# Weight pieces laid out by the host in load order for a two-layer decoder trunk on one core

## The reference

```python
for layer in range(DEPTH):                       # DEPTH = 2
    y = _rmsnorm(h, norm_mix_g[layer])
    h = h + _hybrid_mixer(y, w_in[layer], b_igate[layer], ..., w_out[layer])
    y = _rmsnorm(h, norm_ffn_g[layer])
    if layer % 2 == 0:
        h = h + _swiglu(y, ffn_w_gate[0], ffn_w_up[0], ffn_w_down[0])     # 1024 -> 2752 -> 1024
    else:
        h = h + _moe_swiglu(y, w_router[0], moe_w_gate[0], moe_w_up[0], moe_w_down[0])  # 8 x 1024 -> 3584 -> 1024
return _rmsnorm(h, norm_final_g)

def _swiglu(h, w_gate, w_up, w_down):
    return (jax.nn.silu(h @ w_gate) * (h @ w_up)) @ w_down
```

## Time and profile before

| | |
|---|---|
| median of 3 runs | 1499.48 us (1499.21 to 1503.12) |
| the profiled execution | 1500.5 us, its span 1498.7 us |
| mean granted TensorE clock | 0.989 |
| TensorE busy (matmul) | 1452.7 us, 97% |
| VectorE, ScalarE busy | 1136.4 us (76%), 1005.1 us (67%) |
| HBM read | 434.77 MB |
| SP's queue | 182928 packets, 429.94 MB |

### The profile page before, as it was taken

How to read it: one execution, slowest core, us unless ns; L and a number is a source line. 1 busy time by engine, 2 the same in 40 slices (tenths; PEclk the granted TensorE clock), 3 DMA queues, 4 the chain that set the end, 5 groups by cost and what they waited for, 6 DMA issues and landing times.

```text
span 1498.7 us, 20052 instructions
## 1 busy us (share of the span) xinstructions
PE 1452.7 (97%) x7604; PEld 1237.5 (83%) x7604; DVE 1136.4 (76%) x864; ACT 1005.1 (67%) x827; POOL 33.3 (2%) x62
## 2 busy tenths in 40 slices
PE   5999999999999899999999999999999999999997
PEld 5898899997898688888888888888888888888775
DVE  4456644445455778888888888888888888888997
ACT  4568534435567657777777777777777777777765
POOL 4000000000000010000000000000000000002000
PEclk9999999999999989999999999999999999999999
DMA  9633455554533469999999999999999999999993
GB/s 349 242 115 113 168 171 195 168 183 152 170 114 113 150 252 386 365 377 390 386 371 380 391 367 379 393 370 384 392 373 374 386 376 381 386 375 385 394 365 121
DMA packets 189553, 445.96 MB, mean 298 GB/s; under 512 B 9512, under 2 KB 11560, under 8 KB 189504
## 3 DMA queue, kind: packets, MB, share of 16 engines
q1 hardware_dynamic: 182928, 429.94, 78.9%
q0 software_dynamic: 3344, 11.09, 2.0%
q10 hardware_dynamic: 3232, 4.26, 0.8%
HBM read 434.77 MB, written 10.49 MB: 297 GB/s over the span
## 4 chain that ended last, share of the span: by engine, by line
PE 88%; ACT 4%; DVE 4%; issue 2%; DMA 1%; ACTq 0%; DVEq 0%
PE ps L1374 81%; PE ps L1751 2%; ACT whi L511 2%; DVE wlo L905 1%; DMA wif<-in_w_in_dram 1%; ACT L521 1%; PE ps L1521 1%; PE ps L1393 1%; DVE y L927 0%; PE ps L1721 0%; PE ps L1718 0%; PE ps L1534 0%; DVE y L1092 0%; ACT qkc L685 0%; PE ps L1523 0%
## 5 line engine op out<-in xcount | busy, mean ns | idle before, releaser
L905 DVE TENSOR_TENSOR wlo<-raw,whi 128x2048 fp32r<-128x2048 f32 x405 | 926.1, 2291 | 283.7 <-ACT whi L511 281.8
L511 ACT ACTIVATE whi<-raw 128x2048 fp32r<-128x2048 f32 x405 | 776.9, 1919 | 388.0 <-PE ps L1374 382.6
L1374 PE MATMUL ps<-whi,xT_hi 128*128 128x512 f32 x1056 | 417.7, 396 | 2.2 <-DVE wlo L905 2.2
L1374 PE MATMUL ps<-wlo,xT_hi 128*128 128x512 f32 x1056 | 411.8, 390 | 0.0
L1374 PE MATMUL ps<-whi,xT_lo 128*128 128x512 f32 x1056 | 411.1, 389 | 0.0
L1374 PEld LDWEIGHTS ps<-whi,xT_hi 128*128 128x128 f32 x1056 | 198.4, 188 | 43.0 <-issue 3.2
L1374 PEld LDWEIGHTS ps<-wlo,xT_hi 128*128 128x128 f32 x1056 | 198.2, 188 | 42.4
L1374 PEld LDWEIGHTS ps<-whi,xT_lo 128*128 128x128 f32 x1056 | 198.5, 188 | 38.9
L1374 PE MATMUL ps<-whi,hid_hi 128*128 128x512 f32 (+1 forms) x536 | 210.9, 393 | 0.8 <-DVE hid_lo L1224 0.8
L1374 PE MATMUL ps<-wlo,hid_hi 128*128 128x512 f32 (+1 forms) x536 | 208.9, 390 | 0.0
L1374 PE MATMUL ps<-whi,hid_lo 128*128 128x512 f32 (+1 forms) x536 | 208.8, 389 | 0.0
(11 more groups left out here) (247 smaller groups left out, 776.1 us busy)
## 6 DMA issues: line engine op xcount, KB each, us to landing
raw<-in_moe_w_gate_dram SPq DMA_DIRECT2D x112, 1024.0 KB, 7.4
raw<-in_moe_w_up_dram SPq DMA_DIRECT2D x112, 1024.0 KB, 7.5
raw<-in_moe_w_down_dram SPq DMA_DIRECT2D x112, 1024.0 KB, 7.3
raw<-in_w_in_dram SPq DMA_DIRECT2D x28, 1024.0 KB, 5.6
raw<-in_ffn_w_gate_dram SPq DMA_DIRECT2D x10, 1024.0 KB, 5.1
raw<-in_ffn_w_up_dram SPq DMA_DIRECT2D x10, 1024.0 KB, 5.1
raw<-in_ffn_w_down_dram SPq DMA_DIRECT2D x10, 1024.0 KB, 4.8
raw<-in_w_out_dram SPq DMA_DIRECT2D x8, 1024.0 KB, 4.9
```

The costliest lines, as they stand in the source:

```text
L511: act.activation(whi[:, i % NSPLIT, :], raw[:, i % NRAW, :], ACT.Copy).then_inc(hi_ready, 1)
L905: dve.tensor_tensor(wlo[:, i % NSPLIT, :], raw[:, i % NRAW, :], whi[:, i % NSPLIT, :].bitcast(F32), ALU.subtract).then_inc(lo_ready, 1)
L1374: ins = pe.matmul(acc, lhs, rhs, start=start and m == 0, stop=stop and m == 2, skip_group_check=True)
```

## The change

The host builds one more input, `w_pieces`, of 405 pieces of 128 x 2048 float32 in the order in which they are loaded. Each piece is laid out as the buffer `raw` wants it, so a load reads 128 rows of 8 KB that lie behind one another in HBM. Input `w_in` stays, because `wif` is still cut from it. The output, feed-forward and expert matrices are no longer inputs of the device program. The two short pieces become full ones, and the last piece of the dense layer is loaded by one transfer instead of two.

```diff
-            def load(i, parts):
+            def load(i, at=None):
                 if loop.reg is not None or i >= NRAW:
                     sp.wait_ge(lo_ready, loop.at("piece", i - NRAW + 1))
-                for place, src in parts:
-                    sp.dma_start(place, src).then_inc(arrived[i % NRAW], 16)
-            def cols(i, w, half, c0, n=FB):
-                v = raw[:, i % NRAW, :].rearrange("p (k n) -> p k n", k=4)
-                rows_ = w[half * 512:(half + 1) * 512, bass.ds(c0, n)]
-                load(i, [(v, rows_.rearrange("(k p) n -> p k n", p=P))])
...
+                src = w_pieces[i] if at is None else \
+                    w_pieces[bass.ds(at, 1)].rearrange("o p n -> (o p) n")
+                sp.dma_start(raw[:, i % NRAW, :], src).then_inc(arrived[i % NRAW], 16)
             for t in range(TT):
                 sp.dma_start(h[:, t, :], x[0, t * P:(t + 1) * P, :]).then_inc(x_in[t], 16)
-            mixer(0)
...
-            mixer(1)
+            for i in range(MOE_BASE):
+                load(i)
             def job(e, next_rows=False):
...
+                for i in range(JOB_PIECES):
+                    load(MOE_BASE + i, e * JOB_PIECES + (MOE_BASE + i))
+                    if i == JOB_PIECES // 2 and next_rows:
                         sp.wait_ge(x_sent, 16 * 2 * TT)
                         sp.wait_ge(xg_ps, loop.at("half", 2))
                         sp.dma_start(x_slots, x_by_slot[bass.ds((e + 1) * P, P), :]
...
 def arrival(i, loop):
-    last = FFN_BASE + FFN_PIECES - 1
-    more = 16 if i >= last and (i - last) % NRAW == 0 else 0
-    n = 16 * (i // NRAW + 1) + more
+    n = 16 * (i // NRAW + 1)
...
+def pieces_of(w_in, w_out, ffn_w_gate, ffn_w_up, ffn_w_down, moe_w_gate, moe_w_up, moe_w_down):
+    out = np.zeros((MOE_BASE + E * JOB_PIECES, P, PIECE), np.float32)
+    def cols(i, w, half, c0):
+        out[i].reshape(P, 4, FB)[:] = \
+            w[half * 512:half * 512 + 512, c0:c0 + FB].reshape(4, P, FB).transpose(1, 0, 2)
+    def two_rows(i, w, r0):
+        out[i].reshape(P, 2, D)[:] = w[r0:r0 + 256].reshape(2, P, D).transpose(1, 0, 2)
...
```

More of the change, by code:

```diff
@@ L85, with trunk @@
 DUMP = E * P
-def trunk(nc, x, norm_mix_g, w_in, b_igate, b_fgate, conv_w, conv_b, g_mlstm, g_sb, w_out,
-          norm_ffn_g, ffn_w_gate, ffn_w_up, ffn_w_down, w_router, moe_w_gate, moe_w_up,
-          moe_w_down, norm_final_g, out):
+def trunk(nc, x, norm_mix_g, w_in, w_pieces, b_igate, b_fgate, conv_w, conv_b, g_mlstm, g_sb, norm_ffn_g, w_router,
+          norm_final_g, out):
     x_by_slot = nc.dram_tensor("x_by_slot", (DUMP + 2 * TT * P, D), F32, kind="Internal").ap()
@@ L355, in _ @@
-            load(n, [(v[:, 0], wd[c0:c0 + P, :]), (v[:, 1], wd[F_DENSE - P:, :])])
-            mixer(1)
-            def job(e, next_rows=False):
[L359 to L372, removed]
+            for i in range(MOE_BASE):
+                load(i)
@@ L376, in job @@
                                      ).then_inc(x_slots_in, 16)
-                for half in range(2):
-                    two_rows(n + down_piece(EB - 1, half, EB), expert(moe_w_down),
-                             (EB - 1) * FB + 256 * half)
             with sp.Fori(0, E - 1) as j:
@@ L1840, in arrival @@
 def arrival(i, loop):
-    last = FFN_BASE + FFN_PIECES - 1
-    more = 16 if i >= last and (i - last) % NRAW == 0 else 0
-    n = 16 * (i // NRAW + 1) + more
+    n = 16 * (i // NRAW + 1)
     return n if loop.reg is None else loop.reg * (16 * (loop.per["piece"] // NRAW)) + n
-_INS = ['x', 'norm_mix_g', 'w_in', 'b_igate', 'b_fgate', 'conv_w', 'conv_b', 'g_mlstm', 'g_sb',
-        'w_out', 'norm_ffn_g', 'ffn_w_gate', 'ffn_w_up', 'ffn_w_down', 'w_router', 'moe_w_gate',
-        'moe_w_up', 'moe_w_down', 'norm_final_g']
+def pieces_of(w_in, w_out, ffn_w_gate, ffn_w_up, ffn_w_down, moe_w_gate, moe_w_up, moe_w_down):
+    import numpy as np
+    out = np.zeros((MOE_BASE + E * JOB_PIECES, P, PIECE), np.float32)
[4 more added lines that the diff above has]
+        out[i].reshape(P, 2, D)[:] = w[r0:r0 + 256].reshape(2, P, D).transpose(1, 0, 2)
+    for l in range(DEPTH):
+        for b in range(BLOCKS):
+            for half in range(2):
+                cols(MIX_BASE[l] + 2 * b + half, w_in[l], half, FIRST_COLUMN[b])
+        for i in range(4):
+            two_rows(MIX_BASE[l] + 2 * BLOCKS + i, w_out[l], 256 * OUT_PIECES[i])
+    wg, wu, wd = ffn_w_gate[0], ffn_w_up[0], ffn_w_down[0]
+    for f in range(DENSE_FULL):
+        for half in range(2):
+            cols(FFN_BASE + gate_piece(f, half), wg, half, f * FB)
+            cols(FFN_BASE + gate_piece(f, half) + 2, wu, half, f * FB)
+            if f < DENSE_FULL - 1:
+                two_rows(FFN_BASE + 8 + 6 * f + half, wd, f * FB + 256 * half)
+    n = FFN_BASE + 6 * DENSE_FULL - 2
+    c0 = DENSE_FULL * FB
+    for w in (wg, wu):
+        out[n, :, :KC * TAIL].reshape(P, KC, TAIL)[:] = w[:, c0:].reshape(KC, P, TAIL).transpose(1, 0, 2)
+        n += 1
+    for half in range(2):
+        two_rows(n, wd, c0 - FB + 256 * half)
+        n += 1
+    out[n, :, :D], out[n, :, D:] = wd[c0:c0 + P], wd[F_DENSE - P:]
+    for e in range(E):
+        n = MOE_BASE + e * JOB_PIECES
+        for f in range(EB):
+            for half in range(2):
+                cols(n + gate_piece(f, half), moe_w_gate[0, e], half, f * FB)
+                cols(n + gate_piece(f, half) + 2, moe_w_up[0, e], half, f * FB)
+                two_rows(n + down_piece(f, half, EB), moe_w_down[0, e], f * FB + 256 * half)
+    return out
@@ L1853 @@
+_INS = ['x', 'norm_mix_g', 'w_in', 'w_pieces', 'b_igate', 'b_fgate', 'conv_w', 'conv_b', 'g_mlstm',
+        'g_sb', 'norm_ffn_g', 'w_router', 'norm_final_g']
+_WEIGHTS = ['w_in', 'w_out', 'ffn_w_gate', 'ffn_w_up', 'ffn_w_down', 'moe_w_gate', 'moe_w_up',
+            'moe_w_down']
 def kernel(**inputs):
@@ L1859 @@
     arrays, args = {}, []
+    inputs = dict(inputs)
+    inputs["w_pieces"] = pieces_of(*(np.asarray(inputs[k]) for k in _WEIGHTS))
     for name in _INS:
```

## The result

| | before | after |
|---|---|---|
| median | 1499.51 us (4 runs, 1499.21 to 1503.12) | 1516.92 us (4 runs, 1514.88 to 1517.25) |
| profiled execution, its span | 1500.5 us, 1498.7 us | 1514.88 us, 1513.1 us |

The changed kernel takes 1.0108 times as long (95% interval 1.009 to 1.0126), which is some 16 us; the medians lie 17.4 us apart. The forecast was 1516.

The account below looks back on a forecast made before the run. The start was taken as the bound, where TensorE waits on the chain behind `wif`, not the experts. `wif` 16.6 us late plus 0.5 us of clock made 17.1, 1516.6 from the median 1499.5, stated as 1516; range 1507 to 1521.

Parts of the forecast that it names:

- What bounds the kernel: TensorE is busy throughout the experts, so faster transfers shorten nothing there; the start remains, where the chain waits for `wif`.
- The turn: In the DMA engines: one packet from each busy queue in turn, whatever its size; an 8 KB row as one packet, 0.50.
- the rival of two packets of 4 KB: Each 8 KB row goes as two packets: `wif` 14.6 us late, 15.1 with the clock, 1514.6 us; chance 0.33.
- The price: Start, 7 to 17 us: a turn with an 8 KB packet takes 0.333 us, 30 turns, leaving q10 95 packets per engine.
- the mean engine: Turn arithmetic at the start: an average engine finishes q10's packets at 38.1 us after the change, 20.4 before.
- the tail: Slowest engine at `wif`'s landing: half of the earlier 2.2 us added to 38.1, giving 39.2, so `wif` 16.6 us late.
- The clock: TensorE's restart after a 19 us pause: extra loss bounded by 0 and 1.7 us, taken as 0.5.
- Piece 0: First weight piece at the start: lands 0.3 us sooner, worth nothing because TensorE waits later for piece 1 anyway.
- The store of a job's result: In the experts, on q10: lands 1.9 us later, after 8.1 us, with ScalarE free to wait at 10.3; counted 0.
- The sum: Whole kernel: 16.6 us from late `wif` plus 0.5 of clock, 17.1 us; from the median 1516.6, stated as 1516.
- the first products of the experts: Sign in the profile after: the experts' first 512-column work starts later by the same as TensorE's idle, some 19 us.
- The rival on the faster side: Small queue gets more turns, `wif` lands before about 18 us, no pause after piece 0: 4.5 us gained, 1495.0; chance 0.04.

Follow-up runs that it names:

- two other kernels with a pause of 17 to 18 us: The kernel before with its first seven pieces in 8 KB rows, 1517.41 us; the changed kernel with contiguous pieces in 4 KB rows, 1514.4 us.
- four kernels that do land there: Changed kernel with SP holding from piece 2, 1494.22 us; with first seven pieces in 1 KB rows, 1495.7; with packed `wif`, 1495.27; kernel before with packed `wif`, 1495.14.

## Why the prediction was right

The mechanism held at every step, and the sizes were close; the terms that were off are named below.

*What bounds the kernel.* The experts did not care: an expert's stretch stayed as it was, and loading 398 of 405 pieces in the new way changed nothing that can be told.
*The turn.* One packet of each busy queue in turn, whatever its size: 565 to 566, 229 to 231 to 230. That an 8 KB row is one packet, which no row of before could show, is shown by the count of 59904; the rival of two packets of 4 KB is out, and the run with real 4 KB rows gave the 1514.4 that was worked out for it (1514.6), though its `wif` was used at 36.4 us where I had 37.2, and its clock made up for that.
*The price.* I had q10 with 95 packets left per engine at 17 us; it had (2224 - 222 - 566) / 16 = 90. The turn was 160 / 565 = 0.283 us, not 0.333, and q10 and q1 passed 35 packets per engine in that stretch, not 30. I had left out that each transfer closes with one short packet per engine, so that one in nine of q1's packets is not 8 KB; by my own price that makes 0.30, and the rest of the difference is open. SP's queue, for which I expected some 57,000 packets, had 59904.
But this did not move the landing. Closing packets carry no bulk, and the end is set by the bulk in flight: with 90 left instead of 95 the same arithmetic still empties the mean engine at 38.0 us, not 38.1, since the zeros end at 37.9 either way. The mis-sized term is the tail that I put on top. I took half of the 2.2 us of before, 1.1; `wif` was used 0.4 us after my 38.1. So `wif` came at 38.5 us instead of 39.2, 15.9 late instead of 16.6.
*The clock.* 0.6 us, for 0.5, in the profiled execution. The 0.5 was a choice between 0 and 1.7 and no sum; two other kernels with a pause of 17 to 18 us show 1.1 and 1.2, so that it came so close is in part luck.
*Piece 0* was there 0.5 us sooner (10.43 for 10.94), for 0.3, and it was worth nothing, as said.
*The store of a job's result.* Landing at 9.0 us in the median for 8.1 predicted, and 10.3 us in the slowest of the seven. That is just the cover that the earlier trace rows gave: there ScalarE's next split began 0.17 us late, and TensorE waited for nothing new. It was nearer to costing something than my sum made it.
*The sum.* 15.9 + 0.6 = 16.5 on the chain up to mixer 0's end, 17.4 between the medians, 17.1 predicted. The last 0.9 is inside the scatter of the runs, whose ratio gives some 16 us, and so is the agreement of 17.1 with 17.4. That the first products of the experts would start later by the same did not hold: in the profile it was 13.9 us, as told above.
*The rival on the faster side* was put at 1495.0 for a `wif` that comes before piece 0 ends. The change did not do that, but four kernels that do land there: 1494.2 to 1495.7.

What stays open: why the arithmetic's mean engine was done 2.2 us ahead of the landing before and 0.4 us ahead of it in the changed kernel. The traces divide it in part. Before, q10's last packets were spread out, 5 of them from 21.5 to 22 us and the last after 22.2, and `wif` was used at 22.66; in the changed kernel 113 passed between 37 and 38 us, the last after 37.9, and `wif` was used at 38.54. So the way from the last packet to its use took 0.4 to 0.6 us in both, and what differs lies ahead of the last packet: some 1.8 us before, nothing after.

## What to carry to other kernels

In this kernel a transfer of many short runs cost, per engine, its number of runs times one packet of every other queue that was busy beside it, until the bulk in flight was through: count its runs, look who else is loading, and do it before making anyone's rows longer. Fewer and longer rows could help only where a queue is the bound; here 2 KB rows were enough, 1 KB rows were not, and beyond 2 KB the loads landed a little sooner, which nobody used, and the bystander later. Pack the short runs, or hold the bulk back until they are through: the new layout of 425 MB of weights lost 17 us, and with one wait on SP it is some 6 us faster than the kernel before. That wait was run with 8 KB rows alone, not in the kernel before; with `wif` packed, both layouts are some 5 us faster than the kernel before.

## What the hardware showed that I had not expected

Rows of 1 KB held SP's queue to 350 GB/s with all engines busy (0.047 us each), while rows of 2 KB carried 376 to 387 GB/s in the experts without TensorE waiting for them; the step from "enough" to 4.6% slower is one halving. And a pause of 17 to 19 us did not cost TensorE's clock much more than one of 2.5 us: the 96 products after it took 13.53, 14.02 and 14.13 us against 12.92, 0.6 to 1.2 more. In the run with all but the first seven pieces in 8 KB rows, whose profiled execution paused only 1.6 us, the granted clock did not fall at all (1.00 from 28 to 32 us, where the kernel before had 0.57), and its 96 products took 1.5 us less than 12.92:

```profile
26.71 11.43 PE ps L1326 x96
```
